# State-space input stored unnormed tile by tile in the down half of the MLP and scaled by chunk column; the skip term put into the lag-0 kernels; kernel loads moved

## The reference

```python
x = x + mla(rmsnorm(x))                 # layer 0: latent attention, 16 heads, paged cache for the samples
x = x + sqrelu_mlp(rmsnorm(x))          # w1: 1024 x 4096, w2: 4096 x 1024
x = x + s5(rmsnorm(x))                  # layer 1: state-space mixer, 64 groups of 16 channels, 64 complex states
x = x + sqrelu_mlp(rmsnorm(x))
y = rmsnorm(x)
# s5, for the normed input h, group g:
bu     = b_bar[g] @ h                   # a_bar = exp(dt a), b_bar = (a_bar - 1) / a * b
state  = a_bar * state + bu             # along time; samples start from a given state
out    = Re(c[g] @ state) + d * h       # the skip term
y      = gelu(out) @ w_glu ; mixer = y[:D] * sigmoid(y[D:])
```

## Time and profile before

| | |
|---|---|
| median of 3 runs | 1697.18 us (1695.01 to 1697.72) |
| profiled execution, its own time | 1699.06 us |
| its span in the profile | 1697.1 us |
| mean granted clock of TensorE | 0.955 of full speed |
| PE, DVE, ACT, POOL busy | 90%, 45%, 34%, 19% |
| last down block of the first MLP ends | 1021.5 us from the span's start |
| scan begins, PE goes on after it | 1066.66, 1115.43 |
| first GLU block without waits begins | 1168.15 |

### The profile page before, as it was taken

The page is one execution under the profiler, slowest core; times in us unless marked ns, Lnnn a source line. Parts: engine busy times, 40 slices in busy tenths (PEclk is TensorE's granted clock), DMA queues, the critical chain, the costliest instruction groups (busy, mean ns, idle before and its releaser), DMA issues.

```text
span 1697.1 us, 31652 instructions
## 1 busy us (share of the span) xinstructions
PE 1522.9 (90%) x11310; PEld 1427.9 (84%) x11310; DVE 764.5 (45%) x1133; ACT 584.3 (34%) x1021; POOL 330.4 (19%) x359
## 2 busy tenths in 40 slices
PE   6898888889998999999999993179999999999995
PEld 5866666678887999999999992068999999999995
DVE  3765545545553544423343334644544343344332
ACT  6334434465553333311233221124333321233232
POOL 0274554334320112200123001001002200022000
PEclk9999999989999999999999996679999999999998
DMA  7012222323333222232223928201222222222321
GB/s 170 19 52 71 62 65 69 98 71 103 110 92 103 63 76 86 74 93 80 76 85 90 127 87 217 112 8 51 74 75 86 87 87 76 85 75 86 88 63 56
DMA packets 243227, 142.03 MB, mean 84 GB/s; under 512 B 47127, under 2 KB 237518, under 8 KB 242654
## 3 DMA queue, kind: packets, MB, share of 16 engines
q1 hardware_dynamic: 236898, 133.30, 27.7%
q0 software_dynamic: 5872, 7.78, 2.6%
q10 hardware_dynamic: 396, 0.13, 0.0%
HBM read 126.58 MB, written 14.59 MB: 83 GB/s over the span
## 4 chain that ended last, share of the span: by engine, by line
PE 76%; DVE 6%; issue 6%; DMA 2%; ACT 2%; POOL 1%; POOLq 1%; SPq 0%; DVEq 0%; ACTq 0%
PE bank L819 54%; PE bank L739 5%; PE bank L932 3%; PE bank L1058 3%; PE bank L1023 2%; DMA wraw<-in_mlp_w 2%; PE bank L882 1%; PE bank L1248 1%; PE bank L899 1%; PE bank L1242 1%; PE bank L945 1%; PE bank L939 1%; PE bank L920 1%; ACT arena L1304 1%; DVE arena_parts L1744 1%
## 5 line engine op out<-in xcount | busy, mean ns | idle before, releaser
L819 PE MATMUL bank<-arena_parts,wR 128*128 128x288 f32 x4224 | 568.0, 296 | 8.9 <-DVE wR L1758 4.0
L819 PEld LDWEIGHTS bank<-arena_parts,wR 128*128 128x128 f32 x4224 | 563.5, 188 | 11.3 <-issue 9.1
L819 PE MATMUL bank<-side_parts,wR 128*128 128x288 f32 x3360 | 447.2, 295 | 1.1 <-DVE tmpa L2226 1.1
L819 PEld LDWEIGHTS bank<-side_parts,wR 128*128 128x128 f32 x3360 | 445.3, 188 | 1.5 <-issue 1.3
L1758 DVE TENSOR_TENSOR wR<-wraw,wR 128x1024 fp32r<-128x1024 f32 x159 | 232.8, 1464 | 252.4 <-ACT wR L1367 250.3
L1367 ACT ACTIVATE wR<-wraw 128x1024 fp32r<-128x1024 f32 x159 | 166.9, 1050 | 211.1 <-PE bank L819 192.9
L701 POOL TENSOR_TENSOR arena_parts<-sq,arena_parts 128x576 f32 x64 | 91.6, 1431 | 678.6 <-ACT arena_parts L1584 678.6
L1304 ACT ACTIVATE arena<-bank 128x256 f32<-128x256 f32 (+9 forms) x210 | 92.3, 459 | 167.5 <-PE bank L939 66.1
L1581 ACT ACTIVATE tmpa<-bank 128x576 f32<-128x576 f32 x64 | 41.7, 651 | 195.3 <-PE bank L819 195.3
L2079 DVE TENSOR_TENSOR sq<-tmpa 128x576 f32<-128x576 f32 x64 | 48.6, 759 | 127.1 <-ACT tmpa L1581 127.1
L2065 DVE TENSOR_TENSOR kpR<-bank,rstd 128x576 f32<-128x576 f32 x32 | 24.3, 758 | 136.6 <-PE bank L819 136.6
(11 more groups left out here) (265 smaller groups left out, 1568.3 us busy)
## 6 DMA issues: line engine op xcount, KB each, us to landing
wraw<-in_mlp_w SPq DMA_DIRECT2D x128, 512.0 KB, 4.0
side<-in_cache_ckv SPq DMA_DIRECT2D x128, 128.0 KB, 2.1
wraw<-in_ssm_w_glu SPq DMA_DIRECT2D x16, 512.0 KB, 4.0
s_state_to_out<-side SPq DMA_DIRECT2D x16, 256.0 KB, 2.5
s_in_to_state<-yblk SPq DMA_DIRECT2D x8, 512.0 KB, 3.1
wraw<-in_mla_w_o SPq DMA_DIRECT2D x8, 512.0 KB, 5.1
arena<-s_in_to_state SPq DMA_DIRECT2D x1, 4096.0 KB, 12.2
arena<-s_state_to_out SPq DMA_DIRECT2D x1, 4096.0 KB, 12.5
```

What stands on the lines that cost most here:

```text
L819: return pe.matmul(bank[:, a, 0:HALF], wR[:, s, wp, k, :], tokens(k, xp)[:, a * HALF:(a + 1) * HALF], start=(first and j == 0), stop=(last ...
```

## The change

Seven edits, made together:

1. In the last down half of the first MLP ACT writes each finished tile of `xT`, scaled by the norm's weight alone and steps outermost, to one of two buffers; POOL stores it in `HDR` and loads the inputs of tiles 0 to 5 into `U` (8 transfers a tile); SP loads those of tiles 6 and 7 after the MLP. `U` now lies in `hT`, which is free then.
2. The sum of squares is taken with a sliding window of ones, so that row block r of the result holds the sum for step T-1-r of each chunk: 72 columns instead of 576. DVE multiplies the 8 tiles of `U` by the root mean square's inverse in place. `norm` goes.
3. D goes onto the diagonal of the lag-0 kernels, so the multiply-add after the output transposes goes; GELU reads the bank.
4. `chunk_lags` writes four bands of 32 partitions instead of four column quarters. `KD` rows become 256 long, the first half zeros, so a shifted load brings its zeros and `MI` is not cleared.
5. The 8 kernel loads move from POOL in the down half to SP after the last input-to-state product.
6. `BSTD` is loaded in the down half into `side` (`BS`), where `MI` comes later; `CSD` is loaded into `BC` as soon as the MLP is through.
7. The powers and the window are made by DVE after the fourth down tile.

```diff
-        kdc = side[:, 7552:7552 + QC * P].rearrange("p (q n) -> p q n", q=QC)
+        kdc = side[:, 7552:7552 + 2 * P]
-        U = view(GROUPS * NC).rearrange("p (g c) -> p g c", g=GROUPS)
+        U = flat_h.rearrange("p (g c) -> p g c", g=GROUPS)
+        BS = side[:, 0:2 * GP * P].rearrange("p (a q n) -> p a q n", a=2, q=GP)
+        by_chunk = [ropeq, ropek]
+        window = flat_y[:, 512:512 + 2 * P - GS]
-        KD = nc.dram_tensor("s5_lag_kernels", (GROUPS, GS, P), F32, kind="Internal").ap()
+        KD = nc.dram_tensor("s5_lag_kernels", (GROUPS, GS, 2 * P), F32, kind="Internal").ap()
...
@@ SP, in load_mlp
+                    if (i, half) == (0, 1):
+                        for it in range(4):
+                            load_down(it)
+                            if it == 1:
+                                sp.wait_ge(blk_done, n0)
+                                for a in range(2):
+                                    sp.dma_start(BS[:, a, :, :], BSTD[:, a, :, :]).then_inc(bst_in, 16)
+            def inputs_by_chunk(eng, k, lo, hi):
+                eng.wait_ge(hd_out[k % 2], 16 * (k // 2 + 1))
+                for r in range(lo, hi):
+                    eng.dma_start(U[GS * r:GS * r + GS, 8 * k:8 * k + 8, :],
+                                  HDR[k * P:(k + 1) * P, T - 1 - r, :].rearrange("(g i) c -> i g c", i=GS))\
+                        .then_inc(u_in[1], 16)
...
-            sp.wait_ge(blk_done, B_GLU)
-            sp.dma_start(BC[:, :, :, :], BSTD[:, :, :, :]).then_inc(bst_in, 16)
...
-            for part in range(2):
-                sp.wait_ge(hd_out[part], 16 * 4)
...
-                for r in range(T):
-                    sp.dma_start(U[GS * r:GS * r + GS, gs, :],
-                                 HDR[rows, T - 1 - r, :].rearrange("(g i) c -> i g c", i=GS)).then_inc(u_in[part], 16)
+            inputs_by_chunk(sp, KT - 2, 0, T)
+            inputs_by_chunk(sp, KT - 1, 0, T)
+            sp.wait_ge(blk_done, B_GLU)
+            sp.dma_start(BC[:, :, :, :], CSD[:, :, :, :]).then_inc(cs_in, 16)
             sp.wait_ge(xs_done, 11)
-            sp.dma_start(BC[:, :, :, :], CSD[:, :, :, :]).then_inc(cs_in, 16)
+            for r in range(T):
+                s = T - 1 - r
+                sp.dma_start(MI[GS * r:GS * r + GS, :, :],
+                             KD.rearrange("g i n -> i g n")[:, :, P - GS * s:2 * P - GS * s]).then_inc(mi_in, 16)
@@ POOL
-            pool.wait_ge(blk_done, B_MLP[0] + 48)
-            pool.memset(MI[:, :, :], 0.0).then_inc(mi_zero, 1)
...
-            for r in range(T):
-                s = T - 1 - r
-                pool.dma_start(MI[GS * r:GS * r + GS, :, GS * s:P],
-                               KD.rearrange("g i n -> i g n")[:, :, 0:P - GS * s]).then_inc(mi_in, 16)
-
-            for k in range(KT):
-                pool.wait_ge(h_ready, H_MIX1 + k + 1)
-                pool.dma_start(HDR[k * P:(k + 1) * P].rearrange("p s c -> p (s c)"), hT[:, k, :]).then_inc(hd_out[k // 4], 16)
+            for k in range(KT + 1):
+                if k < KT:
+                    pool.wait_ge(st_ready, k + 1)
+                    pool.dma_start(HDR[k * P:(k + 1) * P].rearrange("p s c -> p (s c)"), by_chunk[k % 2][:, :])\
+                        .then_inc(hd_out[k % 2], 16)
+                if 1 <= k <= KT - 2:
+                    pool.wait_ge(hd_out[(k - 1) % 2], 16 * ((k - 1) // 2 + 1))
+                    for r in range(T):
+                        pool.dma_start(U[GS * r:GS * r + GS, 8 * k - 8:8 * k, :],
+                                       HDR[k * P - P:k * P, T - 1 - r, :].rearrange("(g i) c -> i g c", i=GS))\
+                            .then_inc(u_in[0], 16)
@@ PE, chunk_lags
-                for q in range(QC):
-                    for a in range(2):
-                        ins = pe.matmul(bank7[0:2 * GS, q * P:(q + 1) * P],
+                for a in range(2):
+                    for q in range(QC):
+                        ins = pe.matmul(bank7[2 * GS * q:2 * GS * (q + 1), 0:P],
                                         bbD[:, a, q, :],
@@ PE, after mlp(0)
-            sum_squares(3, Q_MLP1)
+            pe.wait_ge(sq_used, Q_MLP1)
+            acc_by_step = acc.rearrange("p (c s) -> p s c", s=T)
+            for r in range(T):
+                ins = pe.matmul(bank45[:, 0, 0:NC], window[:, P - GS - GS * r:2 * P - GS - GS * r], acc_by_step[:, T - 1 - r, :],
+                                start=(r == 0), stop=(r == T - 1))
+            ins.then_inc(ss_done, 1)
...
-            pe.wait_ge(u_in[0], 16 * T)
+            pe.wait_ge(bst_in, 32)
             for j in range(11):
-                if j == 5:
-                    pe.wait_ge(u_in[1], 16 * T)
+                pe.wait_ge(u_sb, min(3 * j + 2, GP - 1) // 4 + 1)
...
@@ PE, outputs_by_channel
-                    pe.wait_ge(yb_sb, k)
+                    pe.wait_ge(g_sb, k)
@@ ACT, down
                                 act.wait_ge(tile_free, it * 2 + (t0 + j + 1))
+                                if not final:
+                                    t = it * 2 + j
+                                    if t >= 2:
+                                        act.wait_ge(hd_out[t % 2], 16 * (t // 2))
+                                    act.activation(by_chunk[t % 2].rearrange("p (s c) -> p s c", s=T),
+                                                   xT[:, t, :].rearrange("p (c s) -> p s c", s=T), ACT.Identity,
+                                                   scale=vecs[:, V_MIX + 8 + t:V_MIX + 9 + t]).then_inc(st_ready, 1)
@@ ACT
-            root(2)
+            act.activation(rstd[:, 0:NC], rstd[:, 0:NC], ACT.Sqrt).then_inc(rstd_ready, 1)
...
-                act.wait_ge(yb_sb, k + 1)
-                act.activation(hT[:, k, :], hT[:, k, :], ACT.Gelu_apprx_tanh).then_inc(g_sb, 1)
+                act.wait_ge(yb_done, k + 1)
+                act.activation(halves(hT[:, k, :]), bank45[:, :, 0:HALF], ACT.Gelu_apprx_tanh).then_inc(g_sb, 1)
@@ DVE, before and in the pair loop
+            own(dve.tensor_reduce(same[:, :], ident.rearrange("p (j o) -> p o j", o=GS), AX.X, ALU.add))
+            own(dve.memset(kdc[:, 0:P], 0.0))
...
-                dve.tensor_copy(kdc[0:2 * GS, :, :].rearrange("p q n -> p (q n)"), bank7[0:2 * GS, :]).then_inc(kd_sb, 1)
+                dve.scalar_tensor_tensor(out=kdc[:, P:P + GS], in0=same[:, :], scalar=vecs[:, ds(p + V_D, 1)],
+                                         in1=bank7[:, 0:GS], op0=ALU.mult, op1=ALU.add)
+                dve.tensor_copy(kdc[:, P + GS:2 * P], bank7[:, GS:P]).then_inc(kd_sb, 1)
@@ DVE, down half and after it
+            def powers_of_step():
+                dve.wait_ge(blk_done, B_MLP[0] + 48)
...
+                own(dve.memset(window[:, :], 0.0))
+                settle()
+                own(dve.memset(window[:, P - GS:P], 1.0))
+                settle()
...
+                    if (i, half) == (0, 1):
+                        for it in range(4):
+                            down(it)
+                            if it == 1:
+                                powers_of_step()
...
-            norm(3, D, KT, xT, hT, V_MIX + 8, by_token=True)
+            dve.wait_ge(ss_done, 4)
+            own(dve.tensor_scalar(rstd[:, 0:NC], bank45[:, 0, 0:NC], 1.0 / D, EPS, ALU.mult, ALU.add))
             settle()
+            dve.reciprocal(rstd[:, 0:NC], rstd[:, 0:NC]).then_inc(var_ready, 1)
+            dve.wait_ge(rstd_ready, 3)
+            for k in range(KT):
+                if k in (0, KT - 2):
+                    dve.wait_ge(u_in[k // 6], 16 * T * (6 if k == 0 else 2))
+                u = U[:, 8 * k:8 * k + 8, :]
+                tt(u, u, rstd[:, 0:NC].unsqueeze(1).to_broadcast([P, 8, NC]), ALU.mult).then_inc(u_sb, 1)
...
-            for k in range(KT):
-                dve.wait_ge(yb_done, k + 1)
-                dve.scalar_tensor_tensor(out=halves(hT[:, k, :]), in0=halves(hT[:, k, :]),
-                                         scalar=vecs[:, V_D + k:V_D + k + 1], in1=bank45[:, :, 0:HALF],
-                                         op0=ALU.mult, op1=ALU.add).then_inc(yb_sb, 1)
```

More of the change, by code:

```diff
@@ L133, in build @@
         tmpa = sb("tmpa", [P, 2, N])
+        same = sb("same", [P, GS])
         a8 = sb("a8", [P, 3, GP])
@@ L1608, in down @@
                                     tokens_down(it * 2 + j - 1)
-                    if final:
+                    if half == 1:
                         for it in range(4):
@@ L1714, in add_square @@
                 tt(acc[:, :], acc[:, :], sq[:, place, :], ALU.add).then_inc(sq_used, 1)
-            def norm(n, width, tiles, src, dst, v, by_token=False):
-                dve.wait_ge(ss_done, n + 1)
-                own(dve.tensor_scalar(halves(rstd[:, :]), bank45[:, :, 0:HALF], 1.0 / width, EPS, ALU.mult, ALU.add))
-                settle()
-                dve.reciprocal(rstd[:, :], rstd[:, :]).then_inc(var_ready, 1)
-                dve.wait_ge(rstd_ready, 3)
-                for k in range(tiles):
```

(47 more changed lines are left out.)

42 lines of the change are left out of this document (14 added, 28 removed).

## The result

The changed kernel took 1682.37 us in the median of 4 runs (1674.14 to 1684.65), the kernel before 1697.11 beside it; the ratio is 0.9899 with a 95% interval of 0.9877 to 0.9921. So it is faster by 1.0% by the ratio (17 us), and by 14.7 us between the two medians, where 27.7 were forecast. The direction was right; the size is little over half, and the median lies 2.4 us above the upper end of the range. That difference can be split at marks that both timelines have: the key matmuls (line 939 before, 960 now) of the first and of the eighth pair, the first block of the first MLP, its last down block, the first output matmul, the last matmul of all.

A forecast was written before the change was run, and what follows sets the result against it. TensorE, busy 90% of the span, was taken as the bound, standing still mostly at the state-space front. Terms sum to -27.7 us: 1699.06 profiled gives 1671.4, less 1.9 to the runs' median, 1669.5; range 1663 to 1680.

The forecast's parts named there:

- Lag kernels, -6.6: Pair loop: matmuls on four bands run at line 899's pitch, 1.09 us a pair instead of 1.91, over eight pairs.
- rival 2: Lag kernels in the pair loop: four bands overlap fully, saving 11.5 us instead of 6.6, total 1664.6; chance 0.10.
- every tenth taken off line 920 comes off the pair: Pair loop: TensorE's next transposes wait only for the lag-kernel matmuls, so time saved there shortens the pair.
- Down half, +2.4: Last down half of the first MLP: 1.7 us gained by moved loads, 3.1 lost to powers, 1.0 to the clock.
- kernel loads -1.7: Down half: moving these loads out removes TensorE's 1.66 us wait for late weights.
- powers +3.1: Down half, after the fourth down tile: powers on VectorE delay the next cut, a new TensorE wait of about 3.1 us.
- clock +1.0: Down half, after the new wait: a clock drop would cost 1.9 us, taken at an even chance.
- rival 4: Down half: the powers cost 3 us more, with a clock drop and late weights, total 1672.5; chance 0.07.
- Front, -23.2: State-space front: scan starts 21.9 us after the last down block instead of 45.1; bounds on the saving 20 and 24.5.
- Kernel loads, at nothing: Behind the last input matmul: loads take 22 to 42 us, hidden under the scan's 48.8 us.
- rival 3: Scan's end: kernel loads come too late, deciding from 95 ns a row; a little late 0.08 (1677), very late 0.03 (1703).
- Skip term, -0.6: Output stage: the multiply-add between transposes and GELU goes; the chain's end gets 0.6 us shorter.

The follow-up runs named there:

- the bands alone: Kernel before with only the lag kernels' target changed to four 32-partition bands: 1697.67 us, ratio 0.999 to the kernel before.
- the filler: 44 or 45 unused bf16 matmuls a pair where TensorE waits; placed ahead of the key-weight wait: kernel before 1694.40 us (0.9979), changed kernel 1664.73 us (0.9802).
- the powers late: Changed kernel with the powers of the step moved from the down half to behind the eight scalings: 1677.33 us, ratio 0.9867 to the kernel before.
- the other order's profile: Changed kernel with the loops of the lag products exchanged, group by group instead of band after band: 1680.82 us, ratio 0.9892 to the kernel before.
- both edits of the kernel rows: Changed kernel with kernel loads reading aligned rows (1676.98 us), or with each load spread over all 128 partitions (1674.35 us); one run each, wrong output kernels.

## Why the prediction was right and wrong, step by step

- **Lag kernels, -6.6.** The step failed twice. The term was too small: the pitch of line 899 was the wrong row (the 16 matmuls take 0.64 us and not 1.09), and rival 2's size (1.44 a pair) is nearer to the 1.26 measured. The Trainium skill's fourfold column tiling, quoted there, would give 1.91 / 4 = 0.48 us; the rows show 0.57 (start to start) to 0.64, three times and not four. And the sentence "every tenth taken off line 920 comes off the pair" was false for the loop as a whole: the pair got shorter, and TensorE's clock fell more often. With the clock held the whole change gains 1697 x (0.9979 - 0.9802) = 30 us, without it 17 (1 - 0.9899 of 1697), so some 13 us went to the clock, an estimate from two ratios; by the marks of single profiles it is 9.2 in the loop and 3.5 right behind it. That the clock fell more often is shown, by the runs of the bands alone and by the filler that undoes it; what in TensorE's work decides when it falls is not, and other filler than bf16 matmuls was not tried.
- **A clock drop was priced once, and in the wrong place.** I looked for it only where a new wait came (the powers). In the pair loop before it was 0.97, with pauses of PE of 0.6 to 1.3 us in every pair, and I never asked what it does there when PE gets less to do.
- **Down half, +2.4 (kernel loads -1.7, powers +3.1, clock +1.0).** Measured +2.8. The wait was 3.6 for 3.1, since the staging took 1.47 us for 0.7; the drop, put at an even chance, came in this execution and cost 1.3 (in three of six profiles it did not come). That is 4.9 for the 4.1 forecast, 0.8 more and not rival 4's 3. The gain of the loads came as forecast: with the powers gone from it, this stretch takes 463.94 us, 2.2 less than before.
- **Front, -23.2.** Measured -19.4 to the scan: right mechanism, 3.8 too much, just outside the bound of 20. Staging cost 1.33 instead of 0.7; the windowed matmuls ran at a clock of 0.53, 3.54 instead of 2.7; PE started 10.0 us after the block, not 8.8; and from there to the scan it took 15.6 instead of 13.1, of which 1.8 is a gap ahead of the last three steps that nothing in the profile ends. In the other kernels with the new front a gap near that place is 0.4 us in one, 0.8 to 1.0 in four and 1.8 to 2.0 in three; its cause stays open. In the four of 0.8 to 1.0 the scan starts 24.6 to 24.8 us after the block, a gain of 20.3 to 20.5, just inside the bound. Tile 6 was never waited for.
- **Kernel loads, at nothing.** They were 0.55 us late, 0.36 with the powers late and not at all in the other order's profile: rival 3 at its threshold, with 96 ns a row for the 95 at which it decides. What failed is the price of a row: the inputs' 37 ns, grown with the bytes, gave 65, and the highest estimate was 82. The inputs write 16 partitions a transfer too, so the partitions alone don't explain the rest; spreading the rows, or reading them in another order, brought 32 ns.
- **Skip term, -0.6.** The chain from the first output matmul to GLU's blocks is 52.10 instead of 52.72 us: as forecast.
- **Not in the sum: the tail, +3.3.** From the last matmul to the end of the span it is 17.3 us in all the kernels built on the change and 14.0 in all those built on the kernel before. The stores are issued and land alike; the time lies behind them, with no instruction in it. I have not found its cause.
- **Scan.** It took 47.2 us instead of 48.5, also in the profiles of the powers late and of both edits of the kernel rows; not explained.

With the clock held, the same marks in the profiles of before and change with filler give +0.4, -8.9, -1.1, +3.7, -21.4, -1.0 and +3.3: 25.1 us in two single executions, 30 by the medians. The forecast of 27.7 lies between: it was a fair sum of work for a clock that stayed, and it didn't stay.

## What to carry to other kernels

When a cut makes TensorE's share of a loop smaller, read the granted clock of that loop before and after beside the pair's or tile's shortest time: if the shortest iteration gained and the sum didn't, the clock took it, and filler matmuls placed ahead of a wait (not behind it) show this and may give it back. Read the loop in more than one execution: the same seven pairs took 215.5 to 221.9 us in four. Put work that another engine owes early under a wait that exists anyway, as the powers under the input matmuls. And when a transfer's cover is short, don't price its rows by those of a transfer of another shape: these cost 96 ns where the scaled estimate said 65, and 32 when they were spread over all partitions.

## What the runs showed of the hardware

- 16 matmuls of 32 stationary and 128 moving columns took 1.91 us on one band and 0.64 to 0.67 on four, whatever the order of the bands.
- The granted clock of the pair loop was 0.97 before, 0.92 in the change's profile and 0.90 to 0.94 in four others with the same matmuls in the loop, 0.93 with the bands alone, and 0.99 to 1.00 with 44 or 45 filler matmuls a pair. The waits of TensorE in a pair were 0.6 to 1.3 us long.
- Eight loads of 1024 rows of 512 bytes took 49 us into 16 partitions each (89 GB/s) and 16.6 us into 128 in another reading order (290 GB/s). Sixteen loads of 512 rows of 288 bytes, also into 16 partitions each, ran at 146 GB/s.
- After a wait of 3.5 to 3.6 us in the down half TensorE found half clock for 3 us in three profiles and full clock in three.
- ScalarE took 0.67 us to square 128x576 numbers read in order and 1.33 to 1.47 us for the staging, which reads them with a stride of eight numbers; the stride was not tried alone.
